# A two-block transformer kernel: a spare weight buffer at the launch, products at later places, and the growth product two steps earlier

## The reference

```
h = rmsnorm(x); q, k, v, g, u = split(h @ w_in)           # 20 column tiles of 128
y_ret  = silu(g) * head_rmsnorm(retention(rope(q), rope(k), v))     # 4 heads
y_pool = pool_mixer(u)     # 4 groups: windowed mean minus u, then a 128x128 product, then a scale
x = x + concat(y_ret, y_pool) @ w_out                     # first output projection
x = x + cross_attn(rmsnorm(x), rmsnorm(mem)); x = x + conv_glu_ffn(rmsnorm(x))
# second block: gated delta rule over 8 heads, in 64-token chunks, then forgetting attention
o = q*exp(g) @ S + attn @ v_new;   S = S*exp(g_last) + k_dec^T @ v_new     # per chunk
```

## Time and profile before

| what | value |
|---|---|
| time, median of 3 runs (lowest to highest) | 2971.57 us (2971.28 to 2976.7) |
| the profiled execution: its own time / its span | 2975.53 us / 2973.6 us |
| PE busy | 2853.1 us, 96% of the span |
| DVE, ACT, POOL busy | 1499.1, 802.6, 1073.0 us |
| mean granted TensorE clock | 0.981 of full speed |

### The profile page before, as it was taken

The page is one execution under the profiler, slowest core; times in us unless marked ns, Lnnn a source line. Parts: engine busy times, 40 slices in busy tenths (PEclk is TensorE's granted clock), DMA queues, the critical chain, the costliest instruction groups (busy, mean ns, idle before and its releaser), DMA issues.

```text
span 2973.6 us, 35643 instructions
## 1 busy us (share of the span) xinstructions
PE 2853.1 (96%) x14310; PEld 2309.1 (78%) x14310; DVE 1499.1 (50%) x1928; ACT 802.6 (27%) x1164; POOL 1073.0 (36%) x486
## 2 busy tenths in 40 slices
PE   7999999989999999999999999999997999999997
PEld 5887787767788888888878888888785777777776
DVE  6334614123666566556755566666528333334444
ACT  4221302232100000000244433343414433333332
POOL 4222484124334434444422212222236333333235
PEclk9999999999999999999999999999998999999998
DMA  3011231001111111111222212222222111111114
GB/s 140 30 36 71 78 107 50 29 22 50 36 50 48 45 49 42 49 49 42 99 66 74 67 52 67 60 67 60 60 92 85 36 36 36 36 36 42 44 36 151
DMA packets 99158, 173.09 MB, mean 58 GB/s; under 512 B 30640, under 2 KB 60240, under 8 KB 98896
## 3 DMA queue, kind: packets, MB, share of 16 engines
q1 hardware_dynamic: 91312, 144.92, 14.9%
q10 hardware_dynamic: 7200, 24.19, 2.2%
q0 software_dynamic: 512, 2.07, 0.2%
HBM read 152.21 MB, written 18.94 MB: 58 GB/s over the span
## 4 chain that ended last, share of the span: by engine, by line
PE 85%; DVE 6%; POOL 3%; ACT 2%; issue 2%; DMA 1%; ACTq 0%; DVEq 0%; POOLq 0%; SPq 0%
PE gemm L618 19%; PE gemm L619 18%; PE gemm L620 18%; PE small L618 3%; PE small L620 3%; PE small L619 3%; PE small L758 3%; PE small L1295 2%; PE small L1317 2%; PE small L1305 1%; PE small L784 1%; POOL w_lo L531 1%; PE gemm L730 1%; PE small L900 1%; PE small L1158 1%
## 5 line engine op out<-in xcount | busy, mean ns | idle before, releaser
L618 PE MATMUL gemm<-h_hi,w_hi 128*128 128x512 f32 x2560 | 1084.9, 424 | 56.6 <-issue 16.6
L619 PE MATMUL gemm<-h_lo,w_hi 128*128 128x512 f32 x2560 | 1020.9, 399 | 0.0
L620 PE MATMUL gemm<-h_hi,w_lo 128*128 128x512 f32 x2560 | 1019.8, 398 | 0.0
L529 POOL TENSOR_TENSOR w_hi<-w_raw,unit_col 128x1024 fp32r<-128x1024 f32 x180 | 353.0, 1961 | 1513.3 <-PE gemm L620 1289.3
L618 PEld LDWEIGHTS gemm<-h_hi,w_hi 128*128 128x128 f32 x2560 | 488.4, 191 | 169.4 <-issue 39.2
L620 PEld LDWEIGHTS gemm<-h_hi,w_lo 128*128 128x128 f32 x2560 | 486.0, 190 | 119.1
L619 PEld LDWEIGHTS gemm<-h_lo,w_hi 128*128 128x128 f32 x2560 | 488.7, 191 | 100.3 <-issue 6.3
L531 POOL TENSOR_TENSOR w_lo<-w_raw,w_hi 128x1024 fp32r<-128x1024 f32 x180 | 482.7, 2681 | 14.1
L584 POOL TENSOR_TENSOR w_hi<-w_raw,unit_col 128x1024 fp32r<-128x1024 f32 x32 | 60.7, 1896 | 339.7 <-PE gemm L620 339.6
L2319 DVE TENSOR_TENSOR norm<-gemm,norm 128x1024 f32<-128x1024 f32 x44 | 53.8, 1224 | 192.3 <-PE gemm L620 188.5
L618 PE MATMUL small<-act_hi,w_hi 128*128 128x512 f32 x352 | 139.0, 395 | 0.0
(11 more groups left out here) (424 smaller groups left out, 3900.5 us busy)
## 6 DMA issues: line engine op xcount, KB each, us to landing
w_raw<-w_stream SPq DMA_DIRECT2D x201, 512.0 KB, 3.2
x_spill<-xres ACTq DMA_DIRECT2D x16, 512.0 KB, 2.6
xres<-x_t SPq DMA_DIRECT2D x8, 512.0 KB, 8.5
xres<-x_t ACTq DMA_DIRECT2D x8, 512.0 KB, 5.9
xres<-g_rows SPq DMA_DIRECT2D x8, 512.0 KB, 3.7
norm<-g_rows SPq DMA_DIRECT2D x8, 512.0 KB, 3.6
mt_plane<-xres SPq DMA_DIRECT2D x8, 512.0 KB, 3.2
xres<-t_plane SPq DMA_DIRECT2D x8, 512.0 KB, 4.1
```

What stands on the lines that cost most here:

```text
L529: nc.gpsimd.tensor_tensor(whi[d][:, :, :], raw[s][:, :, :], unit, ALU.mult).then_inc(w_hi_done, 1)
L618: mm(dst, w_hi, a_hi, start=first, stop=False)
L619: mm(dst, w_hi, a_lo, start=False, stop=False)
L620: return mm(dst, w_lo, a_hi, start=False, stop=last)
```

## The change

Five things change.

- Launch: two more pairs of split buffers, laid over parts of `head` that are free then. Tile 2 is split into one of them (`W_LAUNCH`) straight after tiles 0 and 1, without a wait for PE. The mixer's squares go to PSUM rather than to `norm`.
- Launch: the angles stand ahead of the reciprocal of the norm on DVE; the spread moves from s = 39 to s = 46 and ACT's copy of it from 39 to 47, behind the sines.
- Pooling: the products of groups 0 and 1 move from s = 28 and 44 to s = 36 and 46.
- Output projection: tile 19 signals each slice of `h_hi` as it is done with it; ACT writes slices 0 to 3 of the mixer's output while tile 19 runs, and DVE makes their rests ahead of group 3's evacuation. Tile 21 is split into the other new pair (`W_MIXED`), straight after tile 20. The pair starts when `gemm0` is free, and its second tile waits for `gemm1`.
- Delta rule: the growth product moves from `level_at(w) + 9` to `level_at(w) + 7` in all windows but the first; the log decays move from s = 24 to s = 21 of window 0.

The diff, cut to its core:

```diff
+        W_LAUNCH, W_MIXED = len(whi), len(whi) + 1
+        whi.extend([w_hi3, w_hi4])
+        wlo.extend([w_lo3, w_lo4])
...
+        MIX_HELD = [0, W_MIXED] + [i % 3 for i in range(2, len(MIX_OUT))]
+        POOL_AT = (36, 46, 60)
...
         def squares(j, k):
+            if j == NMIX:
+                return ps[k % 2][:, :]
...
-            with pool.Fori(1, T_WOUT // 2) as i:
+            split_slot(2, 0, 2, W_LAUNCH)
+            pool.wait_ge(pe_slot, 2)
+            split_slot(3, 1, 2)
+            with pool.Fori(2, T_WOUT // 2) as i:
                 split_pair(i)
             for i in range(len(MIX_OUT)):
                 t = T_WOUT + i
-                if i == 2:
+                if i == 1:
+                    pool.wait_ge(y_done, RET)
+                elif i == 2:
                     pool.wait_ge(h_lo_done, KT * (HRET + 1))
-                if i != 2:
-                    pool.wait_ge(pe_slot, t - 1 if i < 2 else t - 2)
-                split_slot(t, t % 2, t // 2 + 1, i % 3)
+                else:
+                    pool.wait_ge(pe_slot, t - 1 if i < 1 else t - 2)
+                split_slot(t, t % 2, t // 2 + 1, MIX_HELD[i])
...
+                        elif frees and c + w == width:
+                            last.then_inc(h_free, 1)
...
                         if k == 0:
                             pe.wait_ge(w_split, t + b + 1)
+                            if b and second_out is not None:
+                                pe.wait_ge(tile_out, second_out)
...
-                    if w == 0 and s == 39:
+                    if w == 0 and s == 46:
                         pe.wait_ge(norm_rstd, S_MIX + 1)
                         spread(pa, R_H).then_inc(norm_wide, 1)
...
-                    if w == RET and s in (28, 44, 60):
-                        pool_product(s // 16 - 1)
+                    if w == RET and s in POOL_AT:
+                        pool_product(POOL_AT.index(s))
...
-            pe.wait_ge(tile_out, T_WOUT)
+            pe.wait_ge(tile_out, T_WOUT - 1)
...
+            def hi_mixed(k):
+                if k < KT - 1:
+                    act.wait_ge(h_free, k + 1)
+                else:
+                    act.wait_ge(pe_slot, T_WOUT)
+                if k < RET:
+                    act.wait_ge(y_done, k + 1)
+                else:
+                    act.wait_ge(pool_y, k - RET + 1)
+                A(hhi[:, k, :], yt[:, k, :], ACT.Copy).then_inc(h_hi_done, 1)
...
-                    if w == 0 and s == 39:
+                    if w == 0 and s == 47:
                         act.wait_ge(norm_wide, W_MIX + 1)
...
+                    if w == RET and s in (50, 52, 54, 56):
+                        hi_mixed((s - 50) // 2)
...
-            dve.wait_ge(norm_root, NMIX + 1)
-            V.reciprocal(R_H, R_H).then_inc(norm_rstd, 1)
...
             V.tensor_scalar(COS, COS, -1.0, math.pi / 2, ALU.mult, ALU.add).then_inc(angles, 1)
             dve.wait_ge(const_loaded, 64)
+            dve.wait_ge(norm_root, NMIX + 1)
+            V.reciprocal(R_H, R_H).then_inc(norm_rstd, 1)
...
-                if j == 3:
-                    for k in range(4):
-                        lo_part(HRET, k, yt[:, k, :], hhi, hlo)
...
                     if w == RET and s in (20, 36, 52, 68):
+                        if s == 68:
+                            for k in range(RET):
+                                lo_part(HRET, k, yt[:, k, :], hhi, hlo)
                         pool(s // 16 - 1, POOL_WINDOWS[s // 16 - 1])
...
-                if s == level_at(w) + 9:
+                if s == level_at(w) + (9 if w == 1 else 7):
                     dve.wait_ge(gd_growth, g + 1)
                     V.tensor_tensor(N[:, 1, :], N[:, 1, :], yt[:, g, :], ALU.mult).then_inc(gd_qg, 1)
...
+                    if w == 0 and s == 21:
+                        gdn_log_decays()
...
-                    if w == 0 and s == 24:
-                        gdn_log_decays()
```

More of the change, by code:

```diff
@@ L182, in build @@
         xres = sb("xres", [P, KT, S])
+        with nc.sbuf_tensor("head_0", [P, S], F32), nc.sbuf_tensor("w_hi3", [P, KT, P], F32R) as w_hi3, \
+                nc.sbuf_tensor("w_lo3", [P, KT, P], F32R) as w_lo3:
+            pass
+        with nc.sbuf_tensor("head_0_1", [P, 2, S], F32), nc.sbuf_tensor("w_hi4", [P, KT, P], F32R) as w_hi4, \
+                nc.sbuf_tensor("w_lo4", [P, KT, P], F32R) as w_lo4:
+            pass
         H = sb("head", [P, 4, S])
@@ L620, in dot3, with gemm_tile @@
                 return mm(dst, w_lo, a_hi, start=False, stop=last)
-            def gemm_tile(t, b, a_hi, a_lo, width, fresh=None, among=None, s0=0, held=None):
+            def gemm_tile(t, b, a_hi, a_lo, width, fresh=None, among=None, s0=0, held=None, frees=False):
                 d = b if held is None else held
@@ L634, in gemm_tile, with gemm_pair @@
                             last.then_inc(pe_slot, 1)
+                        elif frees and c + w == width:
+                            last.then_inc(h_free, 1)
                         if among is not None:
                             among(s0 + 2 * k + c // HALF)
-            def gemm_pair(t, a_hi, a_lo, fresh, among=None):
+            def gemm_pair(t, a_hi, a_lo, fresh, among=None, held=(0, 1), second_out=None):
                 for k in range(KT):
@@ L644, in gemm_pair @@
                             pe.wait_ge(w_split, t + b + 1)
+                            if b and second_out is not None:
+                                pe.wait_ge(tile_out, second_out)
                         for c in range(2):
                             at = slice(c * HALF, (c + 1) * HALF)
-                            last = dot3(gp[b][:, at], whi[b][:, k, :], wlo[b][:, k, :], a_hi[:, k, at], a_lo[:, k, at],
+                            d = held[b]
+                            last = dot3(gp[b][:, at], whi[d][:, k, :], wlo[d][:, k, :], a_hi[:, k, at], a_lo[:, k, at],
                                         k == 0, k == KT - 1)
@@ L859, in _ @@
                     pe.wait_ge(tile_out, t - 1)
-                    gemm_tile(t, t % 2, hhi, hlo, S, None, among, 16 * j)
+                    gemm_tile(t, t % 2, hhi, hlo, S, None, among, 16 * j, W_LAUNCH if t == 2 else None, t == T_WOUT - 1)
             def pool_last(s):
@@ L882, in _ @@
                 elif kind == "x":
-                    gemm_tile(t, t % 2, hhi, hlo, S, held=i % 3)
+                    gemm_tile(t, t % 2, hhi, hlo, S, held=MIX_HELD[i])
                 else:
-                    gemm_tile(t, t % 2, mem_hi, mem_lo, N_MEM, HMEM if m == 0 else None, held=i % 3)
+                    gemm_tile(t, t % 2, mem_hi, mem_lo, N_MEM, HMEM if m == 0 else None, held=MIX_HELD[i])
                 if i == 0:
@@ L1538, in _ @@
                         A(COS, COS, ACT.Sin).then_inc(rope_tab, 1)
-                    if w == RET and s in (28, 44, 60):
-                        pool_scaled(s // 16 - 1)
+                    if w == RET and s in POOL_AT:
+                        pool_scaled(POOL_AT.index(s))
+                    if w == RET and s in (50, 52, 54, 56):
+                        hi_mixed((s - 50) // 2)
                     if g < 0:
@@ L1563, in _ @@
                         A(R_O, pb[:, 0:NB], ACT.Sqrt, bias=eps[:, 0:1], scale=1.0 / RET_DH).then_inc(y_root, 1)
[L1565 to L1578, removed]
+            for k in range(RET, KT):
+                if k == KT - 1:
+                    act.wait_ge(h_lo_done, KT * HRET + 2)
+                    act.dma_start(memx[:, :, :], mem_t).then_inc(mem_loaded, 16)
+                    pool_scaled(3)
+                    for n in range(5, KT):
+                        act.dma_start(xres[:, n, :], x_t[n]).then_inc(x_loaded[n], 16)
+                hi_mixed(k)
             act.wait_ge(mem_loaded, 16)
```

3 lines of the change are left out of this document (2 added, 1 removed).

## The result

| | kernel before | changed kernel |
|---|---|---|
| time, median (lowest to highest) | 2971.43 us (2971.08 to 2976.7, 4 runs) | 2952.51 us (2951.75 to 2954.81, 4 runs) |
| profiled execution: own time / span | 2975.53 / 2973.6 us | 2951.75 / 2949.8 us |
| PE busy | 2853.1 us | 2841.3 us |
| mean granted clock | 0.981 | 0.985 |

The ratio is 0.9934, with a 95% interval of 0.9916 to 0.9951: the change saves 18.9 us by the medians.

The account below looks back on a forecast made before the run. The prediction took PE, busy 96% of the span, as the bound and read its waits. Terms 3.0 + 3.6 + 4.1 + 2.4 + 1.4 = 14.5 us, taken from 2971.57, gave 2957.1, predicted as 2957, range 2948 to 2967.

Parts of the forecast that it names:

- launch: Start of kernel: tile 2 starts near 38.45 instead of 39.77 and its slow matmuls go; gain 3.0 us.
- pooling and projection: Pooling gets 1.3 us slower by itself, output projection starts earlier; the two stages together gain 3.6, bounds 1.5 to 6.0.
- gates: Delta rule: log decays end at 1526.6, before PE needs them at 1526.9; gain 1.4 us.
- growth product and rest: Delta rule, head of the chain: shorter waits gain 4.1 us in window 3 and 2.4 in windows 4 to 7.
- terms marked (lock): Pooling: DVE and POOL take turns by whole instructions; product 0's small operations end at 284.5, group 2 takes 11.8 us.
- Rival 3: Pooling and projection: DVE's turns fall better, 11.2 us gained there instead of 3.6; total gain 22.1, 2949.5 us; chance 0.10.
- plus 1.6 of clock: Pooling products 0 and 2: the clock falls after each wait, slow matmuls costing 1.6 us more each time.
- The 7.0 us wait: Launch, ahead of the turn of head 0's keys: stays about as long, since the tables meet tile 4's split.
- Rival 1: Delta rule: ACT's copies or the inverse's last level set the later waits; gain 8.0 us, 2963.6; chance 0.11.
- Rival 5: Delta rule: the earlier growth product delays line 2631 and the chain; 18 us slower, 2990; chance 0.05.
- Rival 4: Whole kernel: each shortened wait returns at the next one; gain 0 to 5 us, 2969; chance 0.06.
- Rival 2: Launch and pooling: clock falls after the 1.9 us wait, turns cost 2.4 more; gain 9.3, 2962.3 us; chance 0.09.

## Why the prediction was right, and by how much it missed

I predicted 2957.0 (2948 to 2967) and the median is 2952.5. The waits went, stayed and appeared as all five terms said; one term was mis-sized by slow matmuls that didn't come, and two gains were not in the sum. By the position of the same matmuls in the two profiled executions:

| stretch | forecast | measured | why |
|---|---|---|---|
| launch | 3.0 | 2.8 | tile 2 at 38.73 (forecast 38.45), wait 1.87, key turn at 71.59 (71.2), still 7.04 |
| pooling and projection | 3.6 | 6.4 | waits 2.25 and 2.62 (forecast 2.6 and 2.7), no slow matmuls behind them |
| cross-attention and feed-forward | 0 | 3.8 | granted clock: 2.6 behind the wait at 467.91, 1.1 behind that of 2.74 |
| gates | 1.4 | 1.6 | as forecast |
| behind the gates, to 1557 us | 0 | 1.5 | lower clock gone |
| growth product and rest | 6.5 | 7.7 | waits at line 1090 gone, all of them; 4.4 in window 3 (forecast 4.1) |
| sum | 14.5 | 23.8 | |

- **The lock.** Both terms marked (lock) came as laid out, to 0.4 us at product 0 and 0.1 at product 2, and the 16 columns held for 2.3. Splitting tile 21 later removed the wait at product 2, which shows the cause. Rival 3, without such losses, falls: it was near the measured total (22.1 of 23.8) by other terms. The rule from the Trainium skill, "SBUF — State Buffer", section "SBUF: two separate sides", agrees with these rows.
- **The step that failed** is the term "plus 1.6 of clock", put down for either wait at the products after the earlier trace rows. The waits were there; the falls were not, and these 3.2 cover the 2.8 that the term is off. I had read one row each at 2.74 and 1.78 as a threshold on the length, and the first matmul as the sign of a fall. The second was wrong by rows that I had: the matmul behind the 3.25 us wait takes 0.47, at clock 0.55. The rows of the experiments deny both: the very wait of 2.74 was followed by full clock in two executions of the changed kernel and by the lower one in the third; the wait of 2.62 was followed by 1.98 in two executions of the changed kernel and 3.42 in a third, and by 3.40 in the kernel with tile 4's split late; and even the 1.9 at the launch had a fall once, with a first matmul of 0.50 as without it.
- **What I had at nothing.** In the stages between, the clock gave back 3.8, and behind the gates 1.5. A saving placed ahead of them moves them in time, and what the clock does in them changes, in either direction: 2.7 were lost at the same place in the kernel with later products.
- **The 7.0 us wait** stayed, for the reason given: the tables meet tile 4's split. Moving that split took 2.4 from the wait, and 1.6 from the path. Having the angles done early gave nothing beyond what PE was ahead.
- **Rival 1** fell with the growth product alone. **Rival 5** needed `w_hi` ahead of the product; it took 1.22 in windows 2 to 7 and 1.83 in window 8, and no wait at line 1116 followed. **Rival 4** (gain 0 to 5) fell with 18.9 and 21.5. Rival 2 is half seen: the fall at the launch occurs, in one of three profiled executions of the changed kernel.
- **The reference time.** I counted from 2971.57, a median of three runs. In 56 runs of the experiments its medians were 2976.1 to 2976.5. The changed kernel had 2952.5 and, later, 2954.8. The forecast of 14.5 is thus short of 18.9 by 4.4 and of 21.5 by 7.0. That the time came as near as 4.5 is in part luck: counted from 2976.3, the same 14.5 would have said 2961.8.

## What to carry to other kernels

Price a wait on TensorE by its length, and keep the slow matmuls behind a wait of 1.9 to 2.7 us as a range from nothing to the 1.1 to 2.7 us measured here, not as a yes or no by the length. Before moving work to a later step, look at which tile's end the step lies behind: product 1 at 48 instead of 46 was worth 1.9 to 2.1 us at the pair, as much as the wait that I was after. Where DVE and POOL both work from SBUF, a tiny operation that PE waits for can cost the whole of POOL's instruction; put the split behind it only if nothing later needs the split or DVE's next result as badly, which moved the wait of 2.62 into one of 3.38 here.

## What the runs showed of the hardware

- An operation on 128x16 of DVE took 0.17 alone and 2.30 to 2.38 beside POOL's `w_lo`, in each kernel where it met one; the evacuation from PSUM kept its 1.21 to 1.23. Three operations of 128x1024 beside two splits, with the two small ones, had the rows ready after 11.6; beside one split it took 7.9.
- The granted clock went to its lower level (0.50 in a window, 1.2 of 2.4 GHz) behind some waits of 1.9 to 2.7 us and not behind others of the same length, in one case with the same instructions and waits in two executions of one kernel. Counted over the 14 profiled executions, the clock was at the lower level within 4 us of the end of the wait at tile 2 (1.9 us) in 1 of 9, at product 0 (2.25) in 1 of 6, at product 2 (2.62) in 2 of 5, at the wait of 2.74 in 9 of 14, at the 2.83 of window 3 in 5 of 5, and behind waits of 3.16 to 3.7 in 52 of 53. Around the memory's tile it was so behind the first wait, 3.09, in 8 of 14, and in the other six behind the second, 2.97. So length makes a fall likelier, but isn't all: a wait of 2.38 with one of 1.32 shortly ahead of it (2813.23 us) was followed by the lower level in all 14. Where it fell inside a short tile that a wait follows, it cost nothing; behind that wait it cost 2.7.
- The first matmul behind a wait can take 0.47 to 0.50 and the clock still be low in the microseconds after it; the window shows it, the row doesn't.
